# A decoder layer on one NeuronCore: odd-numbered weight chunks issued from GpSimd's queue instead of SyncE's

## What is computed

```python
h = rmsnorm(x, g_mix_pre)
proj = h @ w_in                      # 2048 x 8208
...                                  # conv, mLSTM chunkwise, rotary, retention chunkwise, head norms, gates
mix = concat(hm, hr) @ w_out         # 2048 x 2048
x = x + rmsnorm(mix, g_mix_post)
h = rmsnorm(x, g_ffn_pre)
ff = (silu(h @ w_gate) * (h @ w_up)) @ w_down
x = x + rmsnorm(ff, g_ffn_post)
```

## Time and profile before

| | before |
|---|---|
| median of 3 runs | 1259.04 us (1252.71 to 1260.53) |
| profiled execution, its device time | 1253.2 us |
| its span from first to last instruction | 1251.5 us |
| mean granted TensorE clock | 0.995 |
| TensorE matmul busy | 1226.7 us (98%) |
| GpSimd busy | 12.4 us (1%) |
| SyncE's queue moved | 226.84 MB |
| GpSimd's queue moved | 2.10 MB |

### The profile page before, as it was taken

One profiled execution on the slowest core, in us unless ns is written; L12 is line 12 of the kernel. 1 busy time (PEld: TensorE's weight loads), 2 busy tenths in 40 slices (PEclk: granted clock), 3 DMA queues, 4 the chain that ended last, 5 costly groups with the idle time before them and its releaser, 6 DMA issues.

```text
span 1251.5 us, 17492 instructions
## 1 busy us (share of the span) xinstructions
PE 1226.7 (98%) x6551; PEld 1052.8 (84%) x6551; DVE 760.4 (61%) x983; ACT 618.4 (49%) x817; POOL 12.4 (1%) x35
## 2 busy tenths in 40 slices
PE   8999989999999999999999999999999999999997
PEld 7788878888888888888888888888888888888886
DVE  5555567767686655766666656656666654444544
ACT  5644557474564644654444454444444443444432
POOL 1000010000000000000000000000000000000000
PEclk9999989999999999999999999999999999999999
DMA  7677687867887555365565565565555565555551
GB/s 207 214 225 149 145 177 163 168 157 157 206 172 189 202 195 188 123 202 192 179 199 187 182 201 180 189 200 176 194 193 181 196 228 185 193 201 194 186 192 67
DMA packets 185925, 229.42 MB, mean 183 GB/s; under 512 B 5920, under 2 KB 145440, under 8 KB 185376
## 3 DMA queue, kind: packets, MB, share of 16 engines
q1 hardware_dynamic: 185600, 226.84, 61.8%
q0 software_dynamic: 288, 2.10, 0.4%
HBM read 226.82 MB, written 2.10 MB: 183 GB/s over the span
## 4 chain that ended last, share of the span: by engine, by line
PE 87%; DMA 7%; DVE 3%; ACT 1%; SPq 1%; issue 1%; DVEq 0%; ACTq 0%
PE bank L1031 86%; DMA raw<-in_w_in 7%; DVE w_lo L646 1%; ACT w_hi L398 1%; DVE h2T L653 0%; DVE resid L924 0%; PE bank L1173 0%; SPq L307 0%; SPq L295 0%; DVE gT L794 0%; DVE gT L804 0%; DVE pre L794 0%; ACT L515 0%; DVE probs L822 0%; DVE h L739 0%
## 5 line engine op out<-in xcount | busy, mean ns | idle before, releaser
L646 DVE TENSOR_TENSOR w_lo<-raw,w_hi 128x1024 fp32r<-128x1024 f32 x424 | 517.5, 1225 | 428.3 <-ACT w_hi L398 425.1
L398 ACT ACTIVATE w_hi<-raw 128x1024 fp32r<-128x1024 f32 x424 | 446.8, 1059 | 519.6 <-PE bank L1031 460.3
L1031 PE MATMUL bank<-h2T,w_hi 128*128 128x512 f32 x1408 | 488.9, 394 | 1.7 <-issue 1.6
L1031 PE MATMUL bank<-h2T,w_lo 128*128 128x256 f32 x1408 | 390.2, 277 | 0.0
L1031 PEld LDWEIGHTS bank<-h2T,w_hi 128*128 128x128 f32 x1408 | 264.0, 188 | 63.8 <-issue 1.8
L1031 PE MATMUL bank<-hT,w_hi 128*128 128x512 f32 x768 | 273.8, 400 | 1.1 <-DVE w_lo L646 1.0
L1031 PEld LDWEIGHTS bank<-h2T,w_lo 128*128 128x128 f32 x1408 | 264.2, 188 | 0.0
L1031 PE MATMUL bank<-w_hi,ffT 128*128 128x512 f32 x704 | 217.0, 389 | 0.0
L1031 PE MATMUL bank<-hT,w_lo 128*128 128x256 f32 x768 | 215.4, 280 | 0.0
L1031 PEld LDWEIGHTS bank<-hT,w_hi 128*128 128x128 f32 x768 | 145.3, 189 | 34.3 <-issue 1.3
L1031 PEld LDWEIGHTS bank<-w_hi,ffT 128*128 128x128 f32 x704 | 132.1, 188 | 27.6
(11 more groups left out here) (159 smaller groups left out, 584.1 us busy)
## 6 DMA issues: line engine op xcount, KB each, us to landing
raw<-in_w_in SPq DMA_DIRECT2D x64, 1024.0 KB, 15.7
raw<-in_w_gate SPq DMA_DIRECT2D x44, 1024.0 KB, 5.1
raw<-in_w_up SPq DMA_DIRECT2D x44, 1024.0 KB, 5.0
raw<-in_w_down SPq DMA_DIRECT2D x44, 1024.0 KB, 5.0
raw<-in_w_out SPq DMA_DIRECT2D x16, 1024.0 KB, 5.2
resid<-in_x SPq DMA_DIRECT2D x2, 1024.0 KB, 6.0
out<-resid SPq DMA_DIRECT2D x8, 256.0 KB, 2.5
g_post<-in_g_mix_post POOLq DMA_DIRECT2D x1, 1024.0 KB, 6.2
```

The costliest lines, as they stand in the source:

```text
L398: act.activation(w_hi[:, s % AHEAD, :], raw[:, s // 2, (s % 2) * SUB:(s % 2 + 1) * SUB], ACT.Copy).then_inc(hi_done, 1)
L646: dve.tensor_tensor(w_lo[:, s % AHEAD, :], raw[:, s // 2, (s % 2) * SUB:(s % 2 + 1) * SUB], w_hi[:, s % AHEAD, :].bitcast(F32), ALU.subtra ...
L1031: return pe.matmul(out_, lhsT, rhs, start=start, stop=stop, skip_group_check=True)
```

## The change

Even chunks (q = 0 and 2) stay in SyncE's queue, in the same loops and with the same waits. Odd chunks (q = 1 and 3) are issued by GpSimd, each written out singly with a constant wait value, for GpSimd has no loop around them. The two odd chunks of round 0 stand ahead of all constants in GpSimd's program, behind a wait for the first half of `x`. Rounds 1 to 3 stand behind the constants. In round 6 the eight heads' masks stand between chunk 1 and chunk 3. The load of `g_post1` stands behind the odd chunks of round 16, that of `g_post2` behind those of round 42. In SyncE's queue `wg` now follows chunk 2 of round 1 directly.

```diff
--- before.py
+++ after.py
@@ -282,6 +282,25 @@
 
             return 4 * group + 2 * part + u
 
+        def rows(w, k0, n, col, width):
+            return w[k0 * P:(k0 + n) * P, bass.ds(col, width)].rearrange("(k p) c -> p k c", p=P)
+
+        def chunk_to(q, src):
+            return raw[:, q, :].rearrange("p (k c) -> p k c", k=src.shape[1])
+
+        def value_rows(r, q):
+            return rows(w_in, 4 * q, 4, 2 * DH + (r % 2) * 512 + (r // 2) * COL_RET, 512)
+
+        def input_rows(kind, half, part, q):
+            return rows(w_in, 8 * (q % 2), 8, COL_RET * kind + 512 * half + (part * DH + (q // 2) * 256), 256)
+
+        def ff_rows(i, q):
+            return rows(w_gate if q < 2 else w_up, 8 * (q % 2), 8, 256 * i, 256)
+
+        def down_rows(n):
+            g, k = divmod(n, KF // 4)
+            return rows(w_down, 4 * k, 4, 512 * g, 512)
+
         block = ctx.enter_context(nc.Block())
 
 
@@ -291,12 +310,7 @@
 
                 if wait:
                     sp.wait_ge(lo_done, 8 * (rnd - 1) + 2 * q + 2)
-                k = src.shape[1]
-                sp.dma_start(raw[:, q, :].rearrange("p (k c) -> p k c", k=k), src)\
-                  .then_inc(raw_full[q], 16)
-
-            def rows(w, k0, n, col, width):
-                return w[k0 * P:(k0 + n) * P, bass.ds(col, width)].rearrange("(k p) c -> p k c", p=P)
+                sp.dma_start(chunk_to(q, src), src).then_inc(raw_full[q], 16)
 
             for t in range(TT):
                 sp.dma_start(resid[:, t, :], x[0, t * P:(t + 1) * P, :]).then_inc(x_in[t], 16)
@@ -316,27 +330,23 @@
             sp.dma_start(cosT[:].bitcast(I32), positions[0:1, :].partition_broadcast(P))\
               .then_inc(small_in, 16)
             for r in range(4):
-                for q in range(4):
-                    col = 2 * DH + (r % 2) * 512 + (r // 2) * COL_RET
-                    load(r, q, rows(w_in, 4 * q, 4, col, 512), wait=r > 0)
+                for q in (0, 2):
+                    load(r, q, value_rows(r, q), wait=r > 0)
                 if r == 1:
                     sp.dma_start(wg[:], rows(w_in, 0, KT, 4 * DH, 2 * HEADS)).then_inc(wg_in, 16)
             with sp.Fori(0, 2) as kind:
                 with sp.Fori(0, 2) as half:
                     for n, part in enumerate((0, 1, 3)):
-                        for q in range(4):
-                            col = COL_RET * kind + 512 * half + (part * DH + (q // 2) * 256)
-                            load(6 * kind + 3 * half + (R_IN + n), q,
-                                 rows(w_in, 8 * (q % 2), 8, col, 256))
+                        for q in (0, 2):
+                            load(6 * kind + 3 * half + (R_IN + n), q, input_rows(kind, half, part, q))
             with sp.Fori(0, 4) as g:
-                for q in range(4):
+                for q in (0, 2):
                     load(g + R_OUT, q, rows(w_out, 4 * q, 4, 512 * g, 512))
             with sp.Fori(0, PAIRS) as i:
-                for q in range(4):
-                    load(i + R_FF, q, rows(w_gate if q < 2 else w_up, 8 * (q % 2), 8, 256 * i, 256))
-            for n in range(4 * KF // 4):
-                g, k = divmod(n, KF // 4)
-                load(R_DOWN + n // 4, n % 4, rows(w_down, 4 * k, 4, 512 * g, 512))
+                for q in (0, 2):
+                    load(i + R_FF, q, ff_rows(i, q))
+            for n in range(0, KF, 2):
+                load(R_DOWN + n // 4, n % 4, down_rows(n))
             for t in range(TT):
                 for c in range(OUT_PARTS):
                     sp.wait_ge(resid_ready, TT * CHUNKS + OUT_PARTS * t + c + 1)
@@ -347,6 +357,15 @@
 
         @block.gpsimd
         def _(pool):
+            def load(rnd, q, src, wait=True):
+
+                if wait:
+                    pool.wait_ge(lo_done, 8 * (rnd - 1) + 2 * q + 2)
+                pool.dma_start(chunk_to(q, src), src).then_inc(raw_full[q], 16)
+
+            pool.wait_ge(x_in[0], 16)
+            for q in (1, 3):
+                load(0, q, value_rows(0, q), wait=False)
             pool.memset(ident, 0.0).then_inc(zeroed, 1)
             pool.memset(sel[:], 0.0).then_inc(zeroed, 1)
             pool.iota(rel[:, 0:2 * P], [[1, 2 * P]], base=0, channel_multiplier=-1,
@@ -370,7 +389,7 @@
             pool.memset(v_sb[:, :, HEADS:2 * HEADS, HD:HD + 1], 0.0).then_inc(consts, 1)
             pool.memset(floor[:, :, HEADS:2 * HEADS], 1.0).then_inc(consts, 1)
 
-            for h in range(HEADS):
+            def mask(h):
                 pool.wait_ge(decay_ready, HEADS + h + 1)
                 for c in (0, 2):
                     block_ = decay[:, h, c * P:(c + 1) * P]
@@ -378,11 +397,38 @@
                                              channel_multiplier=-1)
                 ins.then_inc(masked, 1)
 
+            for r in range(1, 4):
+                for q in (1, 3):
+                    load(r, q, value_rows(r, q))
+            for n, part in enumerate((0, 1, 3)):
+                load(R_IN + n, 1, input_rows(0, 0, part, 1))
+                if n == 2:
+                    for h in range(HEADS):
+                        mask(h)
+                load(R_IN + n, 3, input_rows(0, 0, part, 3))
+            for n, part in enumerate((0, 1, 3)):
+                for q in (1, 3):
+                    load(R_IN + 3 + n, q, input_rows(0, 1, part, q))
+            for half in range(2):
+                for n, part in enumerate((0, 1, 3)):
+                    for q in (1, 3):
+                        load(3 * half + (R_IN + 6 + n), q, input_rows(1, half, part, q))
+            for q in (1, 3):
+                load(R_OUT, q, rows(w_out, 4 * q, 4, 0, 512))
             pool.wait_ge(probs_ready, 2 * HEADS)
             pool.dma_start(g_post1[:], g_mix_post[0:1, :].partition_broadcast(P)).then_inc(post_in, 16)
-
+            for g in range(1, 4):
+                for q in (1, 3):
+                    load(g + R_OUT, q, rows(w_out, 4 * q, 4, 512 * g, 512))
+            for i in range(PAIRS):
+                for q in (1, 3):
+                    load(i + R_FF, q, ff_rows(i, q))
+            for n in (1, 3):
+                load(R_DOWN, n, down_rows(n))
             pool.wait_ge(sub_done, 8 * R_DOWN)
             pool.dma_start(g_post2[:], g_ffn_post[0:1, :].partition_broadcast(P)).then_inc(post_in, 16)
+            for n in range(5, KF, 2):
+                load(R_DOWN + n // 4, n % 4, down_rows(n))
 
 
         @block.scalar
```

## The result

The changed kernel takes 1272.87 us in the median of four runs (1263.08 to 1281.11), the kernel before 1255.88 (1252.65 to 1260.53). The ratio is 1.0161, with a 95% interval from 1.0106 to 1.0216: slower. A second measurement of the same kernel, four runs beside 23 of the kernel before, gave 1262.68 against 1248.74 us, 1.0117 (1.0081 to 1.0152). The profiled execution is the slowest of the first four, 1281.11 us, so its sums are larger than those of the median.

A forecast was written before the change was run, and what follows sets the result against it. TensorE, occupied for 98% of the span, was taken to bound the kernel. Start 5.0 plus masks 0.9 made 5.9 us, 1259.1 from the profiled 1253.2; with 5.8 us for the runs' median, 1265 (own range 1259 to 1272; whole 1252 to 1285).

The forecast's parts named there:

- price of the input rounds: Rounds 4 to 15: bounded between -7.4 and +8 us, taken as zero for the queues and +0.9 for one sure wait.
- The likeliest case: Whole kernel: measured time within about 1% (12.6 us) of the kernel before, chance 0.76.
- the sum: Whole kernel: 5.0 us for the start plus 0.9 for round 6, 5.9 us in all.
- One sign of being wrong: Input rounds: the prediction would be wrong if TensorE lacked more than 15 us there.
- the masks: Round 6: chunk 3 waits in GpSimd's queue until about 162.5 us, 4.6 us late, costing 0.9 us.
- the upper bound: Input rounds: half of ScalarE's 17 waits grow by 5.0 us each, a share of 0.19 reaching TensorE: +8 us.
- My rival on the slow side: Input rounds: odd chunks miss their time, and evenly sharing queues also slow even chunks; 30 us, 1295 us, chance 0.18.
- The share of 0.19: Input rounds: of ScalarE's 59.1 us waiting for w_in chunks, only 11.5 us reached TensorE.
- The price of an issue: GpSimd's queue: issue time proportional to runs, 5.5 ns each, some 2.5 us for 512 runs and 5.0 for 1 KB runs.
- the other bound: GpSimd's queue: issue time independent of the number of runs, 0.54 us each.
- The start: Before the first sub-tile: two GpSimd issues delay ident and line 1100, first sub-tile at 25.7 us; +5.0 us.
- Rounds 1 to 3, the output and the feed-forward rounds: Value rounds 1 to 3, w_out, w_gate, w_up and w_down: no effect; from w_out on, 12 us to spare.

The follow-up runs named there:

- the parts exchanged: Against the kernel before: in rounds 4 to 15 GpSimd issues the even chunks, SyncE the odd ones, masks behind chunk 2 of round 6; 1259.44 us, 1.0095.
- the loads alone: Kernel without computation: eight 1 MB chunks issued at once by one or two engines, run in two orders; w_gate stretches of the first order last 26 to 27 us.
- the one with ScalarE's queue: Against the kernel before: odd chunks of rounds 4 to 15 issued by ScalarE, behind its passes; 1256.55 us, 1.0031 (0.9998 to 1.0064).

## Why the prediction's range held, and its price of the input rounds did not

**The measured time**, 1272.87 us, lies in the whole range (1252 to 1285) and just beyond the forecast's own (1259 to 1272). The likeliest case had been a change within 1%, and it came out slower by 1.6 and 1.2%: 17.0 and 13.9 us by the medians, where the sum was 5.9. That the range held is in part luck: its upper end was set for odd chunks that GpSimd issues too late, and the loss came from even chunks, behind issues that took 0.88 us. One sign of being wrong that the prediction had named did appear: TensorE lacked 20.3 us in the input rounds of the first profile, more than 15. In the second profile it lacked 10.8 us.

**The step that failed** is the price of the input rounds. I bounded it at -7.4 and +8 us and took zero for the queues and 0.9 for the masks. Measured alone it is 13 us by the medians and 15 by the ratio (1.0121), with the parts exchanged 11 and 12 (1.0095), and 10 in the mean of the profiles: above the upper bound by each. The bounds rested on a later issue of the odd chunks. The sentence that failed is "while GpSimd prepares an odd chunk, the even ones have the DMA engines to themselves": preparation is short, and then both queues are loaded, and SyncE's gets one byte in five or six (1.00 of 4.87 MB in the loads alone, 0.20 of 1.19 in the kernel from 98 to 111 us). A chunk that is wanted first is overtaken by its successor, and its landing goes from 24.3 at most to 34.3. My rival on the slow side had named a version of it, two queues that share evenly; an even share came out at 0.3% (up to 0.6 by its interval), the share of four to one at 1.2 and 1.0%. The share of 0.19, by which I turned ScalarE's waits into TensorE's, failed too: ScalarE waited 4.5 us less in total, and TensorE lacked 12.9 us more, for in this profile the longest waits reached it and not their sum. In the profile the way from there is: chunk 2 of round 4 at 131.8, ScalarE and VectorE behind it, TensorE's gap of 8.4 us before 134.33, and the lower granted clock, 0.50, behind the wait. What is shown is that it takes both kinds of queue at once; the size of the packets fits the bytes that each gets, in two ratios, but no run changed it on its own, with all else the same.

The Trainium skill (DMA: Bandwidth & Descriptors, "Queues, rings and completion order") says that a DMA engine goes round the queues that have work, a whole packet from each. By that rule this follows, and the trace agrees: 993 packets each in 14 us. It puts a typical packet at 9 to 17 descriptors; here SyncE's packets are one run of 1 KB (1.18 MB in 1171), so for this queue the measurement decides. Its rule that loads from different issuing engines run on the same 16 DMA engines ("Issuing engines are not separate DMA queues") agrees too: for `w_gate` a pair of queues took 26.3 to 26.7 us, one queue 26.3 to 27.1.

**The price of an issue** was mis-sized: 0.75 us for 512 runs and 0.88 for 1024, where I took 2.5 and 5.0. With 0.54 to 0.70 for 128 runs, an issue is nearly a fixed cost with about 0.25 ns a run on top. The proportional form was wrong, the other bound near. (A slip of no weight stands ahead of it: (27.5 - 16.5)/4 is 2.75 and not 2.72.)

**The start** was right in mechanism and too large: GpSimd began at 6.48 instead of 5.7, two issues took 1.64 us instead of 5.0, line 1100 (now 1146) moved from 10.05 to 16.92 instead of 19.2, the first sub-tile to 23.10 instead of 25.7. The gates' products, the first thing behind round 3, began at 111.01 instead of 107.96, +3.1 us, where I had +5.0. VectorE's scaling begins after the two issues, so whether it can hold them up isn't tested here.

**Rounds 1 to 3, the output and the feed-forward rounds** show no cost: no gap of TensorE in 45.5 to 111, and 1.0022 (0.9986 to 1.0059) for all of it with the start.

**The masks** did hold chunk 3 of round 6, until 175.05 us in GpSimd's order of time, and it still landed, at 185.64, before ScalarE's pass over it at 188.60. The 0.9 us that I gave them is in no measurement:

```profile
173.10 2.00 POOL L396 TENSOR_SCALAR_AFFINE_SELECT decay<-decay 128x128 f32<-128x128 f32 x4 [5.36 <-ACT decay L512]
175.05 0.90 POOL L364 DMA_DIRECT2D raw<-in_w_in  x1
```

**The sum.** By the ratios 2.8 us and 15 us are 18, between the two measurements of the whole, 20 and 15; by the medians 2.1 and 12.8 are 15, between 17.0 and 13.9. The intervals are wide enough that this is no sharp test. Of the first profile's 27.9 us over before, 9.1 lie in the feed-forward rounds and are absent in the second profile of the same kernel; they are the slower pace of the last section, which kernels with one queue show as well in their input rounds.

## What to carry to other kernels

Before a stream of loads is split over two queues, look at the packets of each in the profile: the DMA engines deal them out one for one, so a queue with packets four times as large takes four fifths of the bandwidth while both have work. No harm was seen where a transfer is done long before its data is wanted, as in the feed-forward rounds; it turns the order of arrival around where several are in flight and the one wanted first sits in the queue with small packets. Keep such a stream in one queue, or split it over two of a kind. And where a margin is long, look at the longest landings and at the order of arrival; in the first profile the medians of the landings and the sum of ScalarE's waits fell while the kernel lost time.

## What the runs showed of the hardware that I had not expected

TensorE has two paces for the same products. In the feed-forward rounds of the first profile of the changed kernel a round takes 22.62 us, in the kernel before 22.19, without a gap and at a granted clock of 1.00 in both. The step of line 605 (651 in the changed kernel) marks a round, first in the changed kernel, then in the one before:

```profile
708.33 0.61 ACT L651 ACTIVATE ff_g<-ff_g 128x512 f32<-128x512 f32 x1
...
730.95 0.62 ACT L651 ACTIVATE ff_g<-ff_g 128x512 f32<-128x512 f32 x1
```

```profile
708.83 0.62 ACT L605 ACTIVATE ff_g<-ff_g 128x512 f32<-128x512 f32 x1
...
731.02 0.61 ACT L605 ACTIVATE ff_g<-ff_g 128x512 f32<-128x512 f32 x1
```

Over 22 rounds that is 9 us. The slow pace was there once in two profiles of the changed kernel, in the one with ScalarE's queue (22.61 us a round), and in none of the eight others that compute the layer. Both had two queues in the input rounds, but four other profiles with two had the fast pace; and within the input rounds each of the eleven profiles, those of one queue too, has stretches of either pace (a pair of products 346.7 or 353.3 ns from start to start, 33 to 58% of the pairs at the slower). So a second queue is not what it takes. A product of 512 columns then stands at 399 ns instead of 394, one of 256 at 281 instead of 277. The pace stays through all the rounds of `w_gate` and `w_up`; the eleven rounds of `w_down`, which have the activations as the stationary side, took 239.5 us at either. What picks it is open. It makes two profiles differ by 9 us, and the times of unprofiled runs may hold it too, which no record tells. In the input rounds the slower pairs add up to 1.0 to 2.0 us in every profile, so it moves the table of the input rounds by 1 us at most. The recorded clock doesn't tell the pace either: in the second profile of the changed kernel it stands at 0.95 from 560 to 1007 us, and a round takes 22.19 us, as at 1.00 before.

The input columns of `w_in` are slow to read by every queue and pair that was tried: 8 MB in 1 KB runs took 47 to 54 us with nothing else running, the same in runs of `w_gate` 26 to 27. Rows of `w_in` lie 32,832 bytes apart and those of `w_gate` 22,528; which of their differences makes it was not tried.
